# The last residual taken by tokens, keys' sums 30 steps later, whole tiles in the second feed-forward, and gathers that skip empty places

## The chip, the cores and the metric

One core of a Trainium2 chip runs the whole program in one launch. The time is that of the device, in microseconds (us), from start to end of the program. The kernel before takes 2077.78 us, the median of three runs (2077.6 to 2078.44). Engines: PE (TensorE, matrix products), DVE (VectorE), ACT (ScalarE), POOL (GpSimd), SP (SyncE, which issues nearly all loads).

## The reference

The input is 512 tokens of width 1024 in float32. The first block is attention over chunks, a short convolution, a mixture of 32 experts (two per token, 1024 choices in all) and a gated projection. The second block puts 16 meta tokens in front (528 tokens) and has two layers: a pooling mixer with a feed-forward, then grouped attention over a window with a feed-forward. After the first layer one normed input gives keys and values. What the change touches, cut to it:

```python
# experts: the rows of each expert, in blocks; places without a token have weight 0
xs = xn[row_tok].reshape(n_blk, BLK, d)
hdn = silu(xb @ w1[e]) * (xb @ w3[e]);  ys = hdn @ w2[e]
out = zeros((t, d)).at[row_tok].add(ys * row_w[:, None])

# each layer of the second block ends with
h  = rms_norm_2(hs, norm_ffn_pre[layer])
hs = hs + rms_norm_2(swiglu(h, w_gate_up[layer], w_down[layer]), norm_ffn_post[layer])
# rms_norm_2(y, g) = y / sqrt(mean(y*y) + 1e-6) * g, the mean over the 1024 channels of a token
if layer == 0:
    kv_in = rms_norm_2(hs, kv_norm); k = kv_in @ w_k + b_k; v = kv_in @ w_v + b_v
return hs[:, 16:]
```

Evaluated on its own inputs, the reference gives the 32 experts 50, 36, 28, 41, 36, 37, 32, 34, 20, 24, 25, 29, 27, 23, 26, 28, 44, 38, 29, 34, 37, 39, 31, 22, 35, 32, 28, 44, 28, 28, 26 and 33 of the 1024 choices.

## The kernel before, in words

**Layout.** Activations stand with channels on the 128 partitions and tokens along a row: hT is 8 blocks of 128 channels by 528 tokens. Products are made in three passes of fp32r (`nhi*whi`, `nlo*whi`, `nhi*wlo`), all at L426 in `tile`. One `tile` is one block of 128 output channels: for each of K blocks of inputs it loads a 128x128 weight and multiplies up to 512 tokens into one PSUM bank. In the second block the tokens are held as two halves; in layer 1 these are 256 and 256 tokens (RX), so a tile over both halves takes two banks and two products of 256 columns for each weight.

**Weights.** A unit is 128x1024 (eight 128x128 blocks). SP loads it into one of four raw buffers, ACT casts it to `whi` (L1962), DVE subtracts to get `wlo` (L1130). ACT and DVE do this in `feed`, inside their own copies of the loop over tiles: at block k of tile m, DVE feeds up to the unit in hand plus 2, ACT up to plus 3. A down product with 10 blocks per tile therefore asks for a new unit every 8 blocks.

**Side work.** Each engine has a list of generators (`Side`); `tile` calls `side.tick()` after every block of inputs but the last. So the norms between stages run step by step beside dense products, in an order that is fixed when the program is built: an engine that waits in a side step holds all that stands behind it, its next `feed` too.

**Norm after the downs.** The down products of the second half of the inputs (`fd1`) run for the first token half (r=0, 8 tiles of 10 blocks), then for the second (r=1). After r=0 `after(0)` puts a norm on the list of each engine. `pe_norm` waits a steps, takes the column sums of squares (`columns`, L835 and L836), waits b steps, and spreads the root over the partitions by products with a diagonal (`spread`, L857); (a, b) is LAG = (4, 6). Then 11 steps follow in which DVE scales y by gain and root (L1707), POOL (r=0, L2608) or DVE (r=1, L1712) adds it to hT and, in layer 0, ACT and DVE make `nhi` and `nlo` for the keys while ACT squares and POOL sums (L2547). In layer 0 the sums for the keys' root, `pe_norm("kv", 0, 4, 6)`, stand next on the list: their `columns` come at step 26 counted from the start of r=1.

**The end.** After layer 1, `pe_last` turns hT by 128x128 transposes (L1019) into token rows, ACT copies them out of PSUM (L2500) and SP stores them (L2801), eight stores of 256 KB in pieces of 1 KB. For r=0 this is beside the downs of r=1, for r=1 it is the tail.

**Experts.** Each expert has 64 places. For each pair of experts POOL gathers 128 token rows of 4 KB from HBM by the list `tix` (L2585); a place without a token holds 0, so token 0's row is fetched. SP streams the experts' weights, 96 loads of 2 MB, into nine slots; a slot is loaded again when its products are done. `tix` comes from one-hot products (L604) of `pat` (POOL) and `pb` (DVE), turned to int32 by DVE.

Of the kernel before, what the change touches and what calls it, by code (L numbers as in the profile page):

```python
# [9 lines left out]
ALU = mybir.AluOpType  # L10
# [3 lines left out]
D = 1024  # L14
S = 512
# [34 lines left out]
NRAW = NSP = 4  # L50

# [90 lines left out]
def _program(nc, ctx, T, out, marks):  # L142
# [123 lines left out]
    sl = [pl(f"sl{i}", [128, L]) for i in range(2)]  # L266
    assert pl.off <= nc.sbuf_usable_end
    XW = 4
# [130 lines left out]
    def tensor(e):  # L399
# [473 lines left out]
        def pe_ffn(l, rngs, off, nev, after):  # L873
# [135 lines left out]
        def pe_last(r):  # L1009
            yield from pe_post("fo1", r)  # L1010
            if r == 0:
                for _ in range(WAIT):
                    yield
            for hf in range(2):
                for i in (2 * r, 2 * r + 1):
                    b = take(("fin", i, hf), SIDE)
                    for k in range(4):
                        w.wait_ge(*at("h", "fo1", r, 4 * hf + k))
                        p = e.transpose(b[:, k * 128:(k + 1) * 128],  # L1019
                                        hT[:, 4 * hf + k, MT + i * 128:MT + (i + 1) * 128], ident)  # L1020
                    p.then_inc(*hit("pe_turn", ("turned out", i, hf)))
                    yield
# [33 lines left out]
    WAIT = 10  # L1056
# [12 lines left out]
    LAG = (4, 6)  # L1069
    JOIN = ("join_pe", "join_dve", "join_act", "join_pool", "join_sp")  # L1070
# [47 lines left out]
    def vector(e):  # L1118
# [168 lines left out]
        def dve_route():  # L1287
# [8 lines left out]
            e.tensor_scalar(c31, iota[:, 0:32], -1.0, 31.0, ALU.mult, ALU.add).then_inc(*hit("dve_route"))  # L1296
            w.wait_ge(*at("col", "n2", 0))
# [73 lines left out]
            dv(e.tensor_copy, tix[:], bk("by place", 0, n=NB // 2), ev=[("tix",)])  # L1371
# [10 lines left out]
            for n in range(2):  # L1382
                dv(e.tensor_copy, tcol[:, n, :], bk("by place", n, n=NB // 2), ev=[("free", "by place", n)])
# [295 lines left out]
        def columns(nm, r):  # L1679
# [5 lines left out]
            root(e, w, y, xm, u, "dve_root", nm, r)  # L1685
# [1229 lines left out]
```

## Time and profile before

| What | Value |
|---|---|
| Runs | 2077.6, 2077.78, 2078.44 us |
| The profiled execution's own time | 2076.99 us |
| Its span (first to last instruction) | 2075.2 us |
| Mean granted clock of TensorE | 0.963 |
| PE busy | 1914.2 us (92% of the span) |
| DVE, ACT, POOL busy | 961.8, 651.3, 194.5 us |
| HBM read, written | 349.38 MB, 4.19 MB |

A line of instructions gives a time, a duration, the engine, the line of the kernel, the operation, what it writes and reads with its shape, a count and, in brackets, how long the engine was idle before and what released it. "SPq" or "POOLq" is an engine's issuing queue. A view by stretches gives the busy time of each engine with its instructions, then the granted clock (1.00 is 2.4 GHz, 0.50 is 1.2 GHz), the DMA engines' share and GB/s. The matmuls are pipelined, so the time that one costs in a stream is the distance between two starts, not its duration.

### The profile page before, as it was taken

The page shows a single profiled execution, that of the slowest core. Times are in us where ns is not written, and L with a number is a line of the kernel's source. Part 1 is how long each engine was busy: PE and PEld are TensorE (multiplying, and loading weights), DVE is VectorE, ACT ScalarE, POOL GpSimd, SP SyncE. Part 2 cuts the span into 40 slices and gives each one's busy share as a digit, 9 for nine tenths or more (in the row PEclk, how much of TensorE's full clock was granted, in tenths as well). Part 3 has the DMA queues.
Part 4 walks back from the last instruction along what each step waited for, and adds up shares of the span by engine and source line. Part 5 has one row for each costly group of instructions (what it writes and reads, how often), then busy time and mean ns, then how long its engine had stood idle before and what let it go on. Part 6 is the DMA issues. An engine that isn't in the chain of part 4 may idle for free.

```text
span 2075.2 us, 33252 instructions
## 1 busy us (share of the span) xinstructions
PE 1914.2 (92%) x14370; PEld 1632.3 (79%) x14370; DVE 961.8 (46%) x1702; ACT 651.3 (31%) x1209; POOL 194.5 (9%) x178
## 2 busy tenths in 40 slices
PE   7999999989998898889699999997898789999997
PEld 5766788866665566569699999997766789999996
DVE  5655334223332232257963323357665674323355
ACT  6344323211010010055432222234555543222232
POOL 0011100100000000000300000014122410000012
PEclk9999999989999999999899999998999889999998
DMA  4221243589999999942112322243211333232242
GB/s 178 82 72 61 74 172 102 240 318 426 426 426 426 428 425 426 428 171 82 62 32 92 102 89 75 94 140 102 72 52 41 102 117 117 92 106 87 93 143 82
DMA packets 58087, 355.79 MB, mean 171 GB/s; under 512 B 6304, under 2 KB 8992, under 8 KB 45648
## 3 DMA queue, kind: packets, MB, share of 16 engines
q1 hardware_dynamic: 54112, 340.44, 42.7%
q0 software_dynamic: 3504, 12.73, 1.7%
q8 instruction: 116, 1.90, 0.4%
q10 hardware_dynamic: 320, 0.43, 0.1%
q14 instruction: 35, 0.29, 0.0%
HBM read 349.38 MB, written 4.19 MB: 170 GB/s over the span
## 4 chain that ended last, share of the span: by engine, by line
PE 72%; DVE 10%; DMA 10%; ACT 4%; issue 2%; POOL 2%; SPq 0%; DVEq 0%; ACTq 0%; POOLq 0%
PE bank L426 51%; DMA e<-in_we 9%; PE bank L631 7%; PE bank L653 4%; ACT SS L2442 1%; PE bank L474 1%; PE bank L664 1%; PE bank L780 1%; PE bank L665 1%; DVE wlo L1130 1%; DVE ztmp L1707 1%; POOL zacc L2547 1%; DVE SS L1847 1%; DVE sm L1854 1%; PE bank L618 1%
## 5 line engine op out<-in xcount | busy, mean ns | idle before, releaser
L426 PE MATMUL bank<-nhi,whi 128*128 128x256 f32 (+2 forms) x1472 | 424.9, 289 | 4.1 <-DVE nlo L1717 1.9
L426 PE MATMUL bank<-nhi,wlo 128*128 128x256 f32 (+2 forms) x1472 | 420.1, 285 | 0.0
L426 PE MATMUL bank<-nlo,whi 128*128 128x256 f32 (+2 forms) x1472 | 420.1, 285 | 0.0
L1130 DVE TENSOR_TENSOR wlo<-raw,whi 128x1024 fp32r<-128x1024 f32 x242 | 304.5, 1263 | 131.2 <-ACT whi L1962 127.4
L1962 ACT CAST whi<-raw 128x1024 fp32r<-128x1024 f32 x247 | 256.9, 1043 | 116.4 <-PE bank L426 93.1
L426 PEld LDWEIGHTS bank<-nhi,whi 128*128 128x128 f32 x1472 | 280.0, 190 | 9.1 <-DVE nlo L1717 2.5
L426 PEld LDWEIGHTS bank<-nlo,whi 128*128 128x128 f32 x1472 | 279.6, 190 | 0.9
L426 PEld LDWEIGHTS bank<-nhi,wlo 128*128 128x128 f32 x1472 | 279.1, 190 | 1.5
L631 PE MATMUL bank<-e,xT 128*64 128x256 f32 x2048 | 236.5, 384 | 0.8 <-DVE xT L1392 0.8
L631 PEld LDWEIGHTS bank<-e,xT 128*64 128x64 f32 x2048 | 142.9, 138 | 82.3 <-issue 15.1
L426 PE MATMUL bank<-ghi,whi 128*128 128x256 f32 (+1 forms) x704 | 201.1, 286 | 0.0
L426 PE MATMUL bank<-ghi,wlo 128*128 128x256 f32 (+1 forms) x704 | 199.8, 284 | 0.0
L426 PE MATMUL bank<-glo,whi 128*128 128x256 f32 (+1 forms) x704 | 199.7, 284 | 0.0
L653 PE MATMUL bank<-e,h 128*64 128x256 f32 x1024 | 117.2, 388 | 32.1 <-DMA e<-in_we 31.1
L653 PEld LDWEIGHTS bank<-e,h 128*64 128x64 f32 x1024 | 84.5, 140 | 63.7 <-issue 36.6
L426 PEld LDWEIGHTS bank<-ghi,whi 128*128 128x128 f32 x704 | 134.3, 191 | 0.0
L426 PEld LDWEIGHTS bank<-glo,whi 128*128 128x128 f32 x704 | 134.2, 191 | 0.0
L426 PEld LDWEIGHTS bank<-ghi,wlo 128*128 128x128 f32 x704 | 134.0, 190 | 0.0
L2547 POOL TENSOR_TENSOR zacc<-zacc,zq 128x256 f32<-128x256 f32 (+1 forms) x60 | 59.7, 996 | 775.2 <-ACT zq L2245 774.7
L1414 DVE SCALAR_TENSOR_TENSOR ylo<-bank,tcol,yhi 128x512 fp32r<-128x512 f32 x32 | 23.9, 750 | 233.0 <-ACT yhi L2137 233.0
L426 PE MATMUL bank<-xhi,whi 128*128 128x512 f32 x288 | 122.5, 425 | 0.8 <-DVE xlo L1152 0.8
L426 PE MATMUL bank<-xhi,wlo 128*128 128x512 f32 x288 | 113.7, 395 | 0.0
(343 smaller groups left out, 2969.1 us busy)
## 6 DMA issues: line engine op xcount, KB each, us to landing
e<-in_we SPq DMA_DIRECT2D x96, 2048.0 KB, 34.8
raw<-in_w_down SPq DMA_DIRECT2D x64, 512.0 KB, 3.3
raw<-in_w_gate SPq DMA_DIRECT2D x48, 512.0 KB, 3.3
raw<-in_w_up SPq DMA_DIRECT2D x48, 512.0 KB, 3.2
raw<-in_w_q SPq DMA_DIRECT2D x12, 512.0 KB, 4.4
B<-in_rel POOLq DMA_DIRECT2D x8, 512.0 KB, 4.2
raw<-in_w_gc SPq DMA_DIRECT2D x8, 512.0 KB, 3.3
raw<-in_w_ga SPq DMA_DIRECT2D x8, 512.0 KB, 4.1
```

The costliest lines, as they stand in the source:

```text
L426: i = e.matmul(o, a, x[:, k0 + k, c0:c1], start=(k == 0 and n == 0), stop=(k == j.K - 1 and n == 2))
L474: p = e.matmul(bs[i][:, 0:256], x[:, k, t], a, start=(k == 0 and n == 0), stop=(k == 7 and n == 2))
L618: i = e.transpose(b[:, k * 128:(k + 1) * 128], xg[0 if ov else p % 2][:, (4 * c + k) * 128:(4 * c + k + 1) * 128], ident)
L631: p = e.matmul(b[64 * hf:64 * hf + 64, 0:256], x[:, k, :], W[:, k, 256 * hf:256 * hf + 256], start=(k == 0), stop=(k == 7))
L653: i = e.matmul(b[64 * x:64 * x + 64, 256 * q:256 * q + 256], h2[x][:, 2 * (kc % 2) + kc // 2, :], W[x][:, kc, 512 * nh + 256 * q:512 * nh ...
L664: e.matmul(b[:], yhi[:, k * 128:(k + 1) * 128], pick[:], start=True, stop=False)
L665: e.matmul(b[:], ylo[:, k * 128:(k + 1) * 128], pick[:], start=False, stop=True).then_inc(*hit(f"pe_moe{ov}", ("spread y", p, k)))
L780: p = e.matmul(o, a, x[:, k, c0:c1], start=(k == 0 and n == 0), stop=(k == 7 and n == 2))
L1130: e.tensor_tensor(wlo[wslot(u)][:], raw[u % NRAW][:], whi[wslot(u)][:].bitcast(F32), ALU.subtract).then_inc(*hit("dve_low", ("lo", u)))
L1414: e.scalar_tensor_tensor(ylo[:, c], bk("y", p, nh), tcol[:, 1, p:p + 1], yhi[:, c].bitcast(F32), ALU.mult, ALU.subtract).then_inc(*hit(f"d ...
L1962: e.copy(whi[wslot(u)][:], raw[u % NRAW][:]).then_inc(*hit("act_high", ("hi", u)))
L2547: e.tensor_tensor(a, a, zq[marks.noted("sq", nm, r, k)][:, 0:c1 - c0], ALU.add).then_inc(*hit("pool_acc", ("acc", nm, r, k)))
```

## The change

Five parts.

1. **Empty places.** The list is built from token number minus 1024, and 1024 is added after the sum, so an empty place holds 1024. The gather has a bound of 511 and leaves rows beyond it out. POOL clears both gather buffers once, after `pb`, and the first gather waits for it.
2. **Keys' sums.** `pe_norm("kv", 0, 4, 6)` becomes `(34, 8)` on PE, DVE, ACT and POOL: `columns` at step 56 of the 72 of r=1, `spread` at step 64.
3. **Whole tiles.** In layer 1 the gate and up tiles from the fifth on, and the first downs (`fd0`), run over 512 tokens at once, into one bank. DVE's gate and up steps and ACT's copy of `fd0` are one of 512 instead of two of 256.
4. **h turned early.** During the downs of r=0 in layer 1, PE turns hT (8 groups of four transposes, one group each fifth step) and ACT copies them to `ho` (tokens on partitions).
5. **The sum turned apart.** POOL makes `gdiag`, eight 128x128 diagonals of the gain. PE multiplies y by them (float32), which turns and scales it at once; DVE takes the root as a column only (no diagonal, no spread, no copy of rb) and adds: `ho = turned * root + ho`, 128x512 each. SP stores from `ho` in pieces of 2 KB. DVE's eight scalings, the additions on POOL or DVE and ACT's copies at the end go.

```diff
-                    tile(J["fg", l, i], 0, ("fg", l, i), nhi, nlo, xrs, lambda k: [])
-                    tile(J["fu", l, i], 0, ("fu", l, i), nhi, nlo, xrs, lambda k: [])
+                    tile(J["fg", l, i], 0, ("fg", l, i), nhi, nlo, ALL if l else xrs, lambda k: [])
+                    tile(J["fu", l, i], 0, ("fu", l, i), nhi, nlo, ALL if l else xrs, lambda k: [])
...
-                        tile(J["fd", l, 0, 0], m, ("fd0", l, m), ghi, glo, rr,
+                        tile(J["fd", l, 0, 0], m, ("fd0", l, m), ghi, glo, [(0, (MT, L))] if l else rr,
...
+            if l:
+                side.add(pe_turn_h())
...
-                side.add(pe_norm("kv", 0, 4, 6))
+                side.add(pe_norm("kv", 0, *KV_LAG))
...
-        def pe_last(r):
-            yield from pe_post("fo1", r)
-            if r == 0:
-                for _ in range(WAIT):
-                    yield
-            for hf in range(2):
-                for i in (2 * r, 2 * r + 1):
-                    b = take(("fin", i, hf), SIDE)
+        def pe_turn_h():
+
+            w.wait_ge(*at("out", "fu", 1, 21))
+            for i in range(4):
+                for hf in range(2):
+                    b = take(("h out", i, hf), SIDE)
                     for k in range(4):
-                        w.wait_ge(*at("h", "fo1", r, 4 * hf + k))
+                        w.wait_ge(*at("h", "mp1", i // 2, 4 * hf + k))
                         p = e.transpose(b[:, k * 128:(k + 1) * 128],
                                         hT[:, 4 * hf + k, MT + i * 128:MT + (i + 1) * 128], ident)
+                    p.then_inc(*hit("pe_turn", ("turned h", i, hf)))
+                    yield from nothing(5)
+
+        def pe_last(r):
+
+            def turn(hf):
+                for i in (2 * r, 2 * r + 1):
+                    b = take(("fin", i, hf), DENSE if r and hf else SIDE)
+                    for k in range(4 * hf, 4 * hf + 4):
+                        w.wait_ge(*at("y", "fo1", r, k))
+                        p = e.matmul(b[:, (k % 4) * 128:(k % 4 + 1) * 128], yT[:, k, MT + i * 128:MT + (i + 1) * 128],
+                                     gdiag[:, k, :], start=True, stop=True)
                     p.then_inc(*hit("pe_turn", ("turned out", i, hf)))
-                    yield
+
+            w.wait_ge(*at("gdiag"))
+            if r == 0:
+                yield from nothing(LAG[0])
+            turn(0)
+            yield
+            columns("fo1", r)
+            yield
+            if r == 0:
+                yield from nothing(9)
+            turn(1)
+            yield
...
+    KV_LAG = (34, 8)
...
         def dve_last(r):
-            yield from dve_post("fo1", r, "ffn_post", 1, None, None, 0)
-            for _ in range((WAIT if r == 0 else 0) + 4):
-                yield
+            if r == 0:
+                yield from nothing(LAG[0])
+            yield
+            column_root("fo1", r)
+            yield
+            for hf in range(2):
+                if r == 0 and hf:
+                    yield from nothing(9)
+                for i in (2 * r, 2 * r + 1):
+                    o = ho[:, i, 512 * hf:512 * hf + 512]
+                    w.wait_ge(*at("turned out", i, hf))
+                    w.wait_ge(*at("free", "h out", i, hf))
+                    e.scalar_tensor_tensor(o, bk("fin", i, hf), rcol[:, 0, i + 1:i + 2], o, ALU.mult, ALU.add).then_inc(
+                        *hit("dve_post", ("free", "fin", i, hf)))
+            yield
...
+            w.wait_ge(*at("xg clear"))
...
             e.indirect_dma_start(out=xg[q][:], out_offset=None, in_=n2d,
-                                 in_offset=bass.IndirectOffsetOnAxis(ap=tix[:, p:p + 1], axis=0)).then_inc(
+                                 in_offset=bass.IndirectOffsetOnAxis(ap=tix[:, p:p + 1], axis=0), bounds_check=S - 1,
+                                 oob_is_err=False).then_inc(
                                      *dma(f"d_xg{q}{ov}", ("xg", p)))
...
+        w.wait_ge(*at("pb"))
+        for n in range(2):
+            e.memset(xg[n][:], 0.0).then_inc(*hit("pool_route", *([("xg clear",)] if n else [])))
...
+            if l:
+                g = VEC["ffn_post"] + 8
+                e.tensor_tensor(gdiag[:], ident.unsqueeze(1).to_broadcast([128, 8, 128]),
+                                vec[:, g:g + 8].unsqueeze(2).to_broadcast([128, 8, 128]), ALU.mult).then_inc(
+                                    *hit("pool_post", ("gdiag",)))
...
-                    e.dma_start(out[i * 128:(i + 1) * 128, 512 * hf:512 * hf + 512].rearrange("p (a c) -> p a c", a=2),
-                                out_tile(i, hf)).then_inc(*dma(f"d_out{i}{hf}", ("stored", i, hf)))
+                    e.dma_start(out[i * 128:(i + 1) * 128, 512 * hf:512 * hf + 512],
+                                ho[:, i, 512 * hf:512 * hf + 512]).then_inc(*dma(f"d_out{i}{hf}", ("stored", i, hf)))
```

## Rows read from the trace of the kernel before

**Rows 1.** The page's chain that ended last, by line, shares of the span.
```profile
PE bank L426 51%; DMA e<-in_we 9%; PE bank L631 7%; PE bank L653 4%; ACT SS L2442 1%; PE bank L474 1%; PE bank L664 1%; PE bank L780 1%; PE bank L665 1%; DVE wlo L1130 1%; DVE ztmp L1707 1%; POOL zacc L2547 1%; DVE SS L1847 1%; DVE sm L1854 1%; PE bank L618 1%
```

**Rows 2.** Busy time by stretches of the experts: us, engines, clock, DMA share, GB/s.
```profile
467.00:500.00 33.00, 33.00 (x272) 21.48 (x269) 11.09 (x19) 4.11 (x9) 1.88 (x2) 1.00 1.00 426
...
592.00:860.00 268.00, 240.41 (x1925) 162.20 (x1926) 75.97 (x129) 25.31 (x54) 6.57 (x7) 0.99 1.01 426
```

**Rows 3.** DMA issues: the gathers, their count and median us to landing.
```profile
xg<-n_scratch,tix POOLq DMA_INDIRECT x16, 11.4
```

**Rows 4.** Timeline of the routing's end and a later gather: start us, us, engine, line, what.
```profile
421.37 1.04 POOL L2678 TENSOR_TENSOR scr<-scr,cst 128x512 f32<-128x512 f32 x1 [19.87 <-DVE scr L1291]
...
422.91 0.56 DVE L1291 TENSOR_TENSOR scr<-scr,rows 128x384 f32<-128x384 f32 x1
...
427.30 1.24 POOL L2585 DMA_INDIRECT xg<-n_scratch,tix  x1 [4.89 <-DVE tix L1291]
...
433.13 1.97 PE L618 MATMUL bank<-cst,xg 128*128 128x128 f32 x8 [2.25 <-DMA xg<-n_scratch,tix]
...
496.04 0.94 POOL L2585 DMA_INDIRECT xg<-n_scratch,tix  x1 [26.03 <-PE bank L618]
```

**Rows 5.** Timeline of PE in layer 0's downs, second token half.
```profile
1405.67 0.28 PE L426 MATMUL bank<-ghi,wlo 128*128 128x256 f32 x1
1418.29 0.56 PE L835 MATMUL bank<-cst,zacc 128*128 128x1 f32 x2 [12.34 <-ACT zq L2245]
...
1444.11 0.28 PE L835 MATMUL bank<-cst,zacc 128*128 128x1 f32 x2
```

**Rows 6.** The same stretch on DVE: the next weight unit.
```profile
1418.28 1.22 DVE L1130 TENSOR_TENSOR wlo<-raw,whi 128x1024 fp32r<-128x1024 f32 x1
```

**Rows 7.** Stretches after that stall.
```profile
1418.20:1424.40 6.20, 6.11 (x28) 6.14 (x29) 4.27 (x17) 0.88 (x1) 0.00 (x0) 0.50 0.26 85
```

**Rows 8.** Layer 1's tiles of two halves, a stretch of them.
```profile
1696.00:1840.00 144.00, 144.00 (x1231) 144.00 (x1230) 60.22 (x87) 44.90 (x63) 0.00 (x0) 1.00 0.35 118
```

**Rows 9.** Timeline of PE in products of 512 columns: block 1, then block 2.
```profile
249.66 0.39 PE L426 MATMUL bank<-xhi,whi 128*128 128x512 f32 x1
...
261.90 0.39 PE L426 MATMUL bank<-xhi,whi 128*128 128x512 f32 x1
...
1608.59 0.40 PE L426 MATMUL bank<-nlo,whi 128*128 128x512 f32 x1
...
1619.98 0.39 PE L426 MATMUL bank<-nhi,wlo 128*128 128x512 f32 x1
```

**Rows 10.** Timeline of PE in layer 1's downs, second token half.
```profile
2021.87 0.28 PE L835 MATMUL bank<-cst,zacc 128*128 128x1 f32 x2
...
2025.51 0.71 PE L857 MATMUL bank<-dg,cst 128*128 128x128 f32 x4
2025.97 0.37 PE L426 MATMUL bank<-ghi,whi 128*128 128x256 f32 x1
...
2034.54 0.60 PE L1019 MATMUL bank<-cst,hT 128*128 128x128 f32 x4
2034.89 0.36 PE L426 MATMUL bank<-ghi,whi 128*128 128x256 f32 x1
...
2038.50 0.33 PE L1019 MATMUL bank<-cst,hT 128*128 128x128 f32 x1 [2.00 <-POOL hT L2608]
```

**Rows 11.** Timeline of PE's last dense product and its column sums.
```profile
2057.05 0.28 PE L426 MATMUL bank<-ghi,wlo 128*128 128x256 f32 x1
2058.84 0.35 PE L835 MATMUL bank<-cst,zacc 128*128 128x1 f32 x2 [1.51 <-ACT zq L2245]
```

**Rows 12.** Timeline of DVE and ACT in the tail.
```profile
2062.06 0.43 DVE L1690 TENSOR_TENSOR dg<-cst,rcol 128x256 f32<-128x256 f32 x1
...
2071.63 0.59 ACT L2500 COPY yT<-bank 128x512 f32<-128x512 f32 x1 [0.27 <-PE bank L1019]
```

**Rows 13.** The page's group of DVE's step of 512 columns out of PSUM.
```profile
L1414 DVE SCALAR_TENSOR_TENSOR ylo<-bank,tcol,yhi 128x512 fp32r<-128x512 f32 x32 | 23.9, 750 | 233.0 <-ACT yhi L2137 233.0
```

More of the change, by code:

```diff
@@ L50 @@
 NRAW = NSP = 4
+NOROW = 1024
 class Marks:
@@ L266, in _program @@
     sl = [pl(f"sl{i}", [128, L]) for i in range(2)]
+    gdiag = pl("gdiag", [128, 8, 128])
     assert pl.off <= nc.sbuf_usable_end
+    ho = Place(EA)("ho", [128, 4, D])
     XW = 4
@@ L1370, in dve_route @@
             w.wait_ge(*at("by place", 0))
-            dv(e.tensor_copy, tix[:], bk("by place", 0, n=NB // 2), ev=[("tix",)])
+            dv(e.tensor_scalar, tix[:], bk("by place", 0, n=NB // 2), float(NOROW), None, ALU.add, ev=[("tix",)])
             dv(e.tensor_tensor, R["pw"], pb, wgt[:].rearrange("p a b -> p (a b)").unsqueeze(2).to_broadcast([128, 8, 48]),
@@ L1381, in dve_route @@
             w.wait_ge(*at("by place", 1))
-            for n in range(2):
-                dv(e.tensor_copy, tcol[:, n, :], bk("by place", n, n=NB // 2), ev=[("free", "by place", n)])
+            dv(e.tensor_scalar, tcol[:, 0, :], bk("by place", 0, n=NB // 2), float(NOROW), None, ALU.add,
+               ev=[("free", "by place", 0)])
+            dv(e.tensor_copy, tcol[:, 1, :], bk("by place", 1, n=NB // 2), ev=[("free", "by place", 1)])
         def dve_tokens(p, w, ov=""):
@@ L1677, in mixed_post, with column_root @@
                                                *hit("dve_norm", ("n", "fp0", r, k)))
-        def columns(nm, r):
+        def column_root(nm, r):
             n0, n1 = cols(nm, r)
@@ L1685, in columns @@
             root(e, w, y, xm, u, "dve_root", nm, r)
+            w.wait_ge(*at("root", nm, r))
+        def columns(nm, r):
+            column_root(nm, r)
+            n0, n1 = cols(nm, r)
             m0 = max(n0, 1)
-            w.wait_ge(*at("root", nm, r))
             if n0 == 0:
@@ L1746, in up, with gate_all, up_all @@
                     *hit("dve_out", ("free", *key, r), ("act", l, i, r)))
+            def gate_all(i, key):
+                for r in range(2):
+                    w.wait_ge(*at("free", "rb", nev, r))
+                    if i - 2 < FIRST:
+                        w.wait_ge(*at("g", l, i - 2, r))
+                w.wait_ge(*at("out", *key))
+                if i - 2 >= FIRST:
+                    w.wait_ge(*at("g", l, i - 2))
+                e.tensor_tensor(sl[i % 2][:, t0:t1], bk(*key, 0), rb[:, t0:t1], ALU.mult).then_inc(
+                    *hit("dve_out", ("free", *key, 0), ("gated", l, i, 0), ("gated", l, i, 1)))
+            def up_all(i, key):
+                w.wait_ge(*at("silu", l, i, 0))
+                w.wait_ge(*at("out", *key))
+                e.tensor_tensor(sl[i % 2][:, t0:t1], sl[i % 2][:, t0:t1], bk(*key, 0), ALU.mult).then_inc(
+                    *hit("dve_out", ("free", *key, 0), ("act", l, i, 0), ("act", l, i, 1)))
             def split(i, x0, x1, *r):
@@ L1767, in dve_ffn @@
                     tile(J["fg", l, i], 0)
-                    for r in range(2):
+                    if l:
+                        gate_all(i, ("fg", l, i))
+                    for r in range(0 if l else 2):
                         gate(i, r, ("fg", l, i))
                     tile(J["fu", l, i], 0)
-                    for r in range(2):
+                    if l:
+                        up_all(i, ("fu", l, i))
+                    for r in range(0 if l else 2):
                         up(i, r, ("fu", l, i))
@@ L2366, in act_ffn @@
                         w.wait_ge(*at("out", "fd0", l, m))
-                        for r, (x0, x1) in enumerate(rngs):
+                        for r, (x0, x1) in enumerate([(t0, t1)] if l else rngs):
                             e.copy(yT[:, m, x0:x1], bk("fd0", l, m, r, n=x1 - x0)).then_inc(
@@ L2371, in act_ffn @@
             nm = f"fo{l}"
+            if l:
+                side.add(act_turn_h())
             for r in range(2):
@@ L2488, in act_after1, with act_turn_h @@
         def act_after1(r):
-            side.add(act_last(r))
-        def act_last(r):
-            yield from act_post("fo1", r, None, None, 0)
-            if r == 0:
-                for _ in range(WAIT):
-                    yield
-            for hf in range(2):
-                for i in (2 * r, 2 * r + 1):
-                    w.wait_ge(*at("turned out", i, hf))
-                    w.wait_ge(*at("post x", "fo1", r, 7))
-                    e.copy(out_tile(i, hf), bk("fin", i, hf).rearrange("p (a c) -> p a c", a=2)).then_inc(
-                        *hit("act_out", ("free", "fin", i, hf)))
-                    yield
+            pass
+        def act_turn_h():
+            for i in range(4):
+                for hf in range(2):
+                    w.wait_ge(*at("turned h", i, hf))
+                    e.copy(ho[:, i, 512 * hf:512 * hf + 512], bk("h out", i, hf)).then_inc(
+                        *hit("act_out", ("free", "h out", i, hf)))
+                    yield from nothing(5)
         act_load()
@@ L2631, in pool_after0 @@
             if r == 0:
-                side.add(nothing(11))
+                side.add(nothing(sum(KV_LAG) + 1))
         def pool_kv():
```

18 lines of the change are left out of this document (9 added, 9 removed).

## The prediction

> **What bounds the kernel now.** I read the page's chain first: dense products of PE at L426 hold half of it, the wait for experts' weights 9%, and no group of the other engines over 1% [rows 1]. So a microsecond counts only where it is PE's, the weight stream's, or in the tail. The stretches of the experts show which of the two holds there: the DMA engines are full (share 1.00 and 1.01, 426 GB/s) from 467 us on, while from 592 us PE is idle for 28 of 268 us [rows 2]. In the timeline of PE I then looked for holes: one of 12.34 us before the keys' sums in layer 0 [rows 5], holes before the transposes in layer 1's downs [rows 10], and the tail behind the last dense product [rows 11, 12]. The profiled execution took 2076.99 us, 0.79 less than the median of the runs; the sum is made against it and 0.8 is added at the end.
>
> **1. Empty places.** 16 gathers of 128 rows of 4096 B are 8.39 MB, of which 1024 rows are empty (2048 places, 1024 choices, no expert over its 64). The first three are issued before the stream is full, so 13 count: 13 x 64 rows x 4096 B = 3.41 MB, at 426 GB/s 8.0 us [rows 2, 3]. That is one end, with the missing rows spread evenly over the 16 DMA engines. The other end is 0: if one engine carried only low places, which every expert fills (20 to 50 of 64), it would have as much to do as before, and a load is whole only when its slowest engine is done. I take 6.0 us, nearer to the even case, since on average half of each expert's places fall away but not evenly. PE does not take the bound over: it has 10% of slack there [rows 2], and this takes 2%.
> The Trainium skill (DMA: Bandwidth & Descriptors, The descriptor swizzle) gives the mapping: partitions 4e to 4e+3 and 32 above them go to one engine, the upper 64 partitions to the other eight engines. With the reference's counts the fullest engine would then carry 69 of its 104 rows in those 13 gathers and save 35 x 4096 B at 26.6 GB/s, 5.4 us; no row of this trace tells the engines apart.
>
> The two clears: `pb` is there at 423.5 us (422.91 + 0.56), the first gather is issued at 427.3, so POOL has 3.8 us [rows 4]. Its nearest operation is 1.04 us for 512 elements; twice 1024 would be 4.2 us at that rate and 0.4 late, and a write without reads should be less: 0, bound 0.4. A gather with a bound may cost POOL more or, with half the rows, land sooner than 5.8 us (427.30 to 433.13): 0, bounds -1 to +1; the later ones are issued a pair ahead, some 27 us (0.94 us and 26.03 us of waiting for PE) [rows 4], and hide it. The small edits on DVE stand in its waits: 0.
>
> **2. Keys' sums.** PE stops at 1405.79 (1405.67 and one product of 0.117; step 26, block 29 of 80 of r=1) and goes on at 1418.29 [rows 5]. What it waits for ends late because the 11 steps of scaling, adding, splitting and summing run on DVE, POOL and ACT until 1418.3 whether PE waits or not: the releaser is ACT's square [rows 5]. With `columns` at step 56 PE runs on, but the next thing late is the weight. DVE's `feed` asks for unit 5 of these downs at its own block 24, which stands behind step 21, the last keys' step: it starts at 1418.28, without idle time before it, and takes 1.22 us, ready at 1419.50 [rows 6]. PE needs unit 5 at block 40: 33 more products of 0.117 us [rows 8] bring it there at 1409.65. So the hole shrinks from 12.34 to 9.85 us and moves; it does not go.
> Then, as before, the granted clock is 0.50 for at least 6.2 us after the stall [rows 7]: 30 of the 120 products left cost 0.213 (256 columns at 1.2 GHz), 6.4 us; 90 cost 10.5; the column sums (12 instructions) and the spread 2.1 at full clock. End of r=1: 1419.50 + 19.0 = 1438.5. Before, it ended near 1442.2 (1444.11 less 15 products of 272 columns, 1.9) [rows 5]. Gain 3.7 us; 2.8 if half clock lasts 8 us, 5.2 if 3.5, about half of what is seen. The spread comes 9 blocks, 3.2 us, after sums of 1.3, so 4.5 us from their start; in the tail the diagonal was there 3.7 us from it (2058.84 to 2062.49) [rows 11, 12]: no new wait.
>
> **3. Whole tiles.** 18 gate and 18 up tiles of 8 blocks and 8 downs of 12 blocks, three passes: 864 + 288 = 1152 pairs of 256 columns become products of 512. A pair costs 2 x 0.1170 = 0.2340 us (144 us, 1231 products) [rows 8]. A product of 512 columns cost 0.2267 in block 1 (54 in 12.24 us), but 0.232 over the very operand `nhi` in block 2 (49 in 11.39 us) [rows 9]. I take the latter, as the operand and its spacing stay: 1152 x 0.002 = 2.3 us; ends 1.0 and 8.4. DVE and ACT lose work here, hidden under a PE without holes: 0.
>
> **4. h turned early.** A group of four transposes pushed the next product from 0.117 to 0.35 us behind its start, and that product lasted 0.36 in place of 0.28: 0.43 us [rows 10]. Eight groups beside r=0: +3.4 us on PE. ACT's eight copies (0.59 each [rows 12]) are hidden by PE's 28 us of r=0.
>
> **5. The sum turned apart.** r=1 of layer 1 began at 2020.1 (2021.87 less 15 products) and ended at 2057.17: 37.05 us for 240 products that need 28.1 [rows 10, 11]. In it are the column sums, the spread, four groups of transposes, the waits for POOL's additions and the half clock behind them. After: 28.1, column sums 0.9, and four groups of four float32 products. Such a product is two instructions of 0.115 (2025.51 to 2025.97 for four) [rows 10], so 0.92 + 0.08 a group, 4.0 in all: 33.0, a gain of 4.0. DVE's new steps (root at step 5, additions at 6 and 15) stand before its unit 4 and wait for PE's own steps of the same number, so no weight is late. `gdiag` (128x1024 on POOL) lies in POOL's idle time.
> Tail: before, 15.05 us from 2057.17 to the end of the last copy (2072.22) and 2.98 to the end of the span [rows 12]. After: two turned groups, 16 x 0.115 = 1.84, before the column sums, which so begin 0.3 late (they began at 2058.84); root ready at 2062.35; four additions of 128x512 out of PSUM at 0.75 [rows 13], ended at 2065.35. The other two groups are turned under the root, even at half clock (3.4 us from 2060.0). Then the same 2.98. Gain 6.9; 5.0 if PE is cold and late for the last pair.
>
> **Sum.** -6.0 - 3.7 - 2.3 + 3.4 - 4.0 - 6.9 = -19.5: 2057.5 in the profile's time, 2058.3 us in that of the runs. The terms' own ends: gathers 0 to 8, keys 2.8 to 5.2, whole tiles 1 to 8.4, h 3 to 4, r=1 and tail 8.5 to 11.5.
>
> **Rivals.**
> *The keys' hole goes entirely.* For it: the program puts the sums behind the end of the steps. Against: DVE's order of feeds, worked out above. It would give the hole and its half clock back, some 12 us more: 2046. Chance 0.10.
> *The gathers save nothing.* For it: a row left out may still cost its engine a descriptor, or one engine keeps all its rows. Against: counts around half. 2058.3 + 6 = 2064.3. Chance 0.17.
> *Slower: the bound makes the gather dear.* If POOL's gather with a bound checks row by row, its landing could grow from 5.8 to over 26 us. The first would hold up PE and the weights' slots for the excess in full; later ones hide up to 15 us (27 less 11.4) [rows 3, 4]. From 20 us of excess on, the change is not faster: 2079. For it: POOL builds the list in software and the trace has no gather of this form; against: a whole gather now keeps POOL 0.94 to 1.24 us [rows 4]. Chance 0.04.
> *Whole tiles at block 1's pace* (0.2267): 6 us more, 2052. Chance 0.12. The forecast itself has 0.57.
>
> **Numbers.** 2058.3; range 2049 to 2067, which leaves out most of the first rival and of the slow one, and holds both disputed sizes. No difference means within 0.2%, 4 us. Faster 0.94, same 0.02, slower 0.04.
>
> **What would show it.** A hole of about 10 us at block 40 of layer 0's r=1 whose releaser is DVE's L1130 in place of 12.3 before L835; 0.232 us a product in layer 1; half the gathered rows and a stream that ends some 6 us sooner after its start; no wait for POOL in layer 1's downs; 11 us from the last dense product to the end in place of 18. Wrong would be: another releaser or no hole at all in layer 0, PE waiting for `xg` beyond the first, or a wait for `gdiag` or `turned out` in front of a weight feed.

## Result and the profile after

The kernel after takes 2051.35 us (median of 4 runs, 2050.37 to 2057.19), the kernel before 2078.11 beside it (4 runs); ratio 0.9877, 95% interval 0.986 to 0.9894. The forecast was 2058.3 (2049 to 2067). The profiled execution took 2052.12 us with a span of 2050.3, 24.9 less than before's.

The page's chain that ended last, by line (L429, L634 and L656 are before's L426, L631 and L653), and its line on the queue of the gathers (packets, MB, share of 16 engines):

```profile
PE 75%; DVE 10%; DMA 8%; ACT 4%; issue 2%; POOL 1%; DVEq 0%; SPq 0%; ACTq 0%; POOLq 0%
PE bank L429 52%; PE bank L634 8%; DMA e<-in_we 7%; PE bank L656 4%; ACT SS L2512 1%; PE bank L667 1%; PE bank L477 1%; PE bank L668 1%; PE bank L783 1%; DVE wlo L1157 1%; DVE SS L1903 1%; DVE sm L1910 1%; PE bank L621 1%; POOL zacc L2608 1%; PE bank L494 1%
...
q0 software_dynamic: 3504, 8.54, 1.2%
```

The weights' share of the chain fell from 9 to 7% [rows 1]. The queue moves 4.19 MB less than the 12.73 of before, in the same 3504 packets: a row left out is still a small packet.

**Experts.** The stretch that answers to [rows 2] (us, engines, clock, DMA share, GB/s), the routing's end in the timeline [rows 4], and what PE waited for from 440 to 910 us, first in the kernel after, then before (us in total, times, longest):

```profile
592.00:860.00 268.00, 248.81 (x1970) 165.17 (x1968) 77.75 (x133) 25.54 (x54) 6.93 (x7) 0.97 1.01 426
```
```profile
422.93 1.04 POOL L2746 TENSOR_TENSOR scr<-scr 128x512 f32<-128x512 f32 x1 [19.85 <-DVE scr L1318]
425.09 1.85 POOL L2751 MEMSET xg<- 128x1024 f32 x2 [1.11 <-DVE scr L1318]
429.44 1.10 POOL L2647 DMA_INDIRECT xg<-n_scratch,tix  x1 [2.50 <-DVE scr L1318]
...
434.87 1.54 PE L621 MATMUL bank<-cst,xg 128*128 128x128 f32 x6 [2.43 <-DMA xg<-n_scratch,tix]
```
```profile
PE bank L656 <- DMA e<-in_we: 21.3, 8, 4.4
```
```profile
PE bank L653 <- DMA e<-in_we: 31.1, 10, 4.9
```

The DMA engines stay full at 426 GB/s, so the stream still sets the time, but it has less to carry: PE waits 9.8 us less. The clears end at 426.94, 2.5 us before the gather: they cost nothing. The gather's issue is 2.14 us later than before's, of which 1.56 were there at `pat` already. The other 0.58 stand on POOL between `tix` and the issue: `tix` was ready at 428.57 (427.02 before), 0.87 us ahead of the gather in place of 0.28. From issue to PE it takes 5.4 us (5.8 before), from `tix` to PE 6.3 (6.1), so the bound is not dear.

**Keys' sums.** PE and DVE around the stall [rows 5, 6], and the stretch behind it [rows 7]:

```profile
1405.58 0.28 PE L429 MATMUL bank<-ghi,wlo 128*128 128x256 f32 x1
...
1415.42 0.55 PE L429 MATMUL bank<-ghi,whi 128*128 128x256 f32 x1 [9.56 <-DVE wlo L1157]
```
```profile
1413.63 0.50 DVE L1751 SCALAR_TENSOR_TENSOR nlo<-hT,vec,nhi 128x272 fp32r<-128x272 f32 x1 [1.20 <-ACT nhi L2382]
1414.05 1.22 DVE L1157 TENSOR_TENSOR wlo<-raw,whi 128x1024 fp32r<-128x1024 f32 x1
```
```profile
1415.40:1418.90 3.50, 3.48 (x17) 3.50 (x18) 3.43 (x6) 2.15 (x4) 1.50 (x2) 0.53 0.66 173
```

The hole is where the forecast put it, behind DVE's low part of unit 5, which stands behind the last step for the keys. The half clock behind it lasted 3.5 us here, 6.2 or more before.

**Layer 1.** The whole tiles, then the second downs' two halves, before and after [rows 8, 10], and a group of h's transposes:

```profile
1722.39:1991.88 269.49, 269.49 (x2307) 269.49 (x2306) 94.44 (x137) 73.77 (x100) 0.00 (x0) 1.00 0.29 97
1991.88:2020.12 28.24, 28.24 (x242) 28.24 (x241) 18.82 (x27) 13.59 (x18) 7.24 (x6) 1.00 0.52 171
2020.12:2057.17 37.05, 33.61 (x270) 32.93 (x268) 24.47 (x44) 12.60 (x20) 14.82 (x14) 0.95 0.29 98
```
```profile
1708.62:1975.55 266.93, 266.93 (x1155) 216.37 (x1153) 92.17 (x102) 73.31 (x92) 0.00 (x0) 1.00 0.32 97
1975.55:2007.35 31.80, 31.80 (x274) 31.80 (x273) 18.83 (x26) 17.80 (x26) 7.25 (x6) 1.00 0.51 151
2007.35:2040.05 32.70, 32.70 (x283) 32.70 (x282) 20.34 (x39) 10.15 (x15) 6.29 (x6) 1.00 0.34 112
```
```profile
1975.91 0.60 PE L1022 MATMUL bank<-cst,hT 128*128 128x128 f32 x4
1976.26 0.36 PE L429 MATMUL bank<-ghi,whi 128*128 128x256 f32 x1
1976.46 0.28 PE L429 MATMUL bank<-glo,whi 128*128 128x256 f32 x1
```

1152 products in 266.93 us are 0.2317 each. A group takes 0.55 us in place of one product's 0.12 (1975.91 to 1976.46): 0.43, eight times. In the last stretch PE is busy throughout, at full clock, where before it idled 3.4 us.

**Tail.** PE, DVE and the stores [rows 11, 12]:

```profile
2040.05 1.95 PE L1034 MATMUL bank<-gdiag,yT 128*128 128x128 f32 x16
2041.83 0.28 PE L838 MATMUL bank<-cst,zacc 128*128 128x1 f32 x2
...
2042.64 2.03 PE L1034 MATMUL bank<-gdiag,yT 128*128 128x128 f32 x16
```
```profile
2044.98 2.73 DVE L1980 SCALAR_TENSOR_TENSOR ho<-bank,rcol,ho 128x512 f32<-128x512 f32 x4
```
```profile
out<-ho SPq DMA_DIRECT2D x4, 256.0 KB, 2.1
```

10.26 us from the last dense product's end at 2040.05 to the span's end, in place of 18.02.

**The ledger.** Dense products are counted in PE's order, so both programs can be cut at the same ones. Lengths in us, each from the starts of two products in the profile (the last from the last product's end to the span's end):

| stretch | before | after | difference | forecast |
|---|---|---|---|---|
| to product 504 (block 1) | 227.45 | 229.03 | +1.58 | 0 |
| routing and experts, to 1248 | 679.31 | 672.50 | -6.81 | -6.0 |
| to 1776 (layer 0's gates) | 130.88 | 131.86 | +0.98 | 0 |
| to 4548 | 362.05 | 362.03 | -0.02 | 0 |
| layer 0's downs, second half, to 4752 | 42.52 | 37.98 | -4.54 | -3.7 |
| keys and attention of layer 1, to 5100 | 169.66 | 165.36 | -4.30 | 0 |
| to the first whole tile | 110.52 | 109.86 | -0.66 | 0 |
| whole tiles | 269.49 | 266.93 | -2.56 | -2.3 |
| second downs, first half | 28.24 | 31.80 | +3.55 | +3.4 |
| second downs, second half | 37.05 | 32.70 | -4.35 | -4.0 |
| behind the last dense product | 18.02 | 10.26 | -7.76 | -6.9 |

The changed stretches sum to -22.5, those that nothing changed in to -2.4. Of the latter, attention is the large one. There the clock tells. The whole stretch of the keys and attention, before and after:

```profile
1442.21:1611.87 169.66, 151.47 (x1006) 116.74 (x1005) 105.33 (x234) 90.64 (x258) 35.30 (x26) 0.94 0.16 57
```
```profile
1433.40:1598.76 165.36, 145.86 (x1006) 112.39 (x1005) 105.15 (x234) 90.45 (x258) 35.30 (x26) 0.98 0.19 58
```

By these clocks PE was at half clock for some 20 us of it before and for 7 after. Two stretches of before at part clock, and the one after that answers to the second:

```profile
1486.00:1506.00 20.00, 17.11 (x82) 10.82 (x82) 11.67 (x30) 11.96 (x38) 4.24 (x3) 0.74 0.08 27
1600.00:1607.00 7.00, 6.06 (x30) 5.04 (x30) 1.08 (x4) 3.41 (x8) 1.90 (x1) 0.51 0.01 2
```
```profile
1586.00:1596.00 10.00, 7.15 (x60) 5.51 (x59) 2.89 (x9) 5.79 (x17) 1.89 (x1) 1.00 0.13 49
```

The same stall stands in both just ahead of the second, before and after:

```profile
1600.94 1.98 PE L976 MATMUL bank<-PT,V 128*64 128x128 f32 x16 [2.86 <-ACT PT L2431]
```
```profile
1590.67 1.09 PE L981 MATMUL bank<-PT,V 128*64 128x128 f32 x16 [2.85 <-ACT PT L2501]
```

Before, half clock follows it and costs 2.8 us, after it does not. Why is open.

### The profile page after: what moved, and what is told of

Read it like the earlier page. It is cut to its first block, busy times and chain, and to the rows that moved or that the text cites. A ratio compares the mean times of both kernels' runs of the same rounds, so it can differ in the third digit from the quotient of the medians.

```text
span 2050.3 us, 30975 instructions
## 1 busy us (share of the span) xinstructions
PE 1909.2 (93%) x13274; PEld 1576.3 (77%) x13274; DVE 952.0 (46%) x1649; ACT 649.9 (32%) x1199; POOL 190.0 (9%) x173
## 3 DMA queue, kind: packets, MB, share of 16 engines
q0 software_dynamic: 3504, 8.54, 1.2%
HBM read 349.38 MB, written 4.19 MB: 172 GB/s over the span
## 4 chain that ended last, share of the span: by engine, by line
PE 75%; DVE 10%; DMA 8%; ACT 4%; issue 2%; POOL 1%; DVEq 0%; SPq 0%; ACTq 0%; POOLq 0%
PE bank L429 52%; PE bank L634 8%; DMA e<-in_we 7%; PE bank L656 4%; ACT SS L2512 1%; PE bank L667 1%; PE bank L477 1%; PE bank L668 1%; PE bank L783 1%; DVE wlo L1157 1%; DVE SS L1903 1%; DVE sm L1910 1%; PE bank L621 1%; POOL zacc L2608 1%; PE bank L494 1%
## 5 line engine op out<-in xcount | busy, mean ns | idle before, releaser
L429 PE MATMUL bank<-nhi,whi 128*128 128x256 f32 (+2 forms) x1184 | 375.8, 317 | 3.7 <-DVE yT L1955 1.6
L429 PE MATMUL bank<-nlo,whi 128*128 128x256 f32 (+2 forms) x1184 | 372.9, 315 | 0.0
L429 PE MATMUL bank<-nhi,wlo 128*128 128x256 f32 (+2 forms) x1184 | 372.8, 315 | 0.0
L429 PEld LDWEIGHTS bank<-nhi,whi 128*128 128x128 f32 x1184 | 225.4, 190 | 21.6 <-DVE nlo L1751 2.2
L634 PE MATMUL bank<-e,xT 128*64 128x256 f32 x2048 | 237.0, 385 | 0.8 <-DVE xT L1422 0.8
L429 PEld LDWEIGHTS bank<-nlo,whi 128*128 128x128 f32 x1184 | 225.0, 190 | 13.6
L429 PEld LDWEIGHTS bank<-nhi,wlo 128*128 128x128 f32 x1184 | 224.8, 190 | 13.6
L634 PEld LDWEIGHTS bank<-e,xT 128*64 128x64 f32 x2048 | 143.2, 138 | 82.5 <-issue 14.9
L429 PE MATMUL bank<-ghi,whi 128*128 128x272 f32 (+2 forms) x608 | 184.7, 304 | 9.6 <-DVE wlo L1157 9.6
L429 PE MATMUL bank<-ghi,wlo 128*128 128x272 f32 (+2 forms) x608 | 183.4, 302 | 0.0
L429 PE MATMUL bank<-glo,whi 128*128 128x272 f32 (+2 forms) x608 | 183.4, 302 | 0.0
L656 PE MATMUL bank<-e,h 128*64 128x256 f32 x1024 | 119.5, 393 | 22.5 <-DMA e<-in_we 21.3
L1444 DVE SCALAR_TENSOR_TENSOR ylo<-bank,tcol,yhi 128x512 fp32r<-128x512 f32 x32 | 23.9, 750 | 225.6 <-ACT yhi L2205 225.6
L656 PEld LDWEIGHTS bank<-e,h 128*64 128x64 f32 x1024 | 83.7, 142 | 57.0 <-issue 29.6
L429 PEld LDWEIGHTS bank<-ghi,whi 128*128 128x128 f32 x608 | 115.4, 190 | 14.3 <-issue 9.7
L429 PE MATMUL bank<-xhi,whi 128*128 128x512 f32 x288 | 123.1, 427 | 0.9 <-DVE xlo L1179 0.9
L429 PEld LDWEIGHTS bank<-glo,whi 128*128 128x128 f32 x608 | 115.3, 190 | 4.3
L429 PEld LDWEIGHTS bank<-ghi,wlo 128*128 128x128 f32 x608 | 115.1, 189 | 4.1
L429 PE MATMUL bank<-xhi,wlo 128*128 128x512 f32 x288 | 114.4, 397 | 0.0
```

Of the source, the lines that this page charges most:

```text
L429: i = e.matmul(o, a, x[:, k0 + k, c0:c1], start=(k == 0 and n == 0), stop=(k == j.K - 1 and n == 2))
L634: p = e.matmul(b[64 * hf:64 * hf + 64, 0:256], x[:, k, :], W[:, k, 256 * hf:256 * hf + 256], start=(k == 0), stop=(k == 7))
L656: i = e.matmul(b[64 * x:64 * x + 64, 256 * q:256 * q + 256], h2[x][:, 2 * (kc % 2) + kc // 2, :], W[x][:, kc, 512 * nh + 256 * q:512 * nh ...
L1444: e.scalar_tensor_tensor(ylo[:, c], bk("y", p, nh), tcol[:, 1, p:p + 1], yhi[:, c].bitcast(F32), ALU.mult, ALU.subtract).then_inc(*hit(f"d ...
```

## Experiments

Each run's time is the median, beside before's on the same chip. The ratio and its interval are estimated from all executions and can lie 0.2% off the quotient of the two medians. Since the executions of one kernel differ by up to 10.7 us, the stretches of the profiles carry the verdicts; each of these is one execution.

**Each part alone, on the kernel before.** The edits are the diff's own hunks, one part in each kernel.

> The kernel before with part 1 alone (rows for empty places left out, the bound, the clears). Theory (the weight stream sets the time of the experts, and rows not moved shorten it): last expert product 6 to 7 us sooner, less 0.2 to 2 us of a later first gather; 2071.5 against 2078.1. Rival (the gain of the profile after in the experts, 6.8 us from its start, comes from somewhere else, or a row left out still costs its engine): under 2 us, 2076 to 2078. In both the rest of the program keeps its distances, except for half-clock phases of TensorE, which may fall elsewhere.

> The kernel before with part 2 alone (column sums for the keys at step 56 and spread at 64). Theory: the hole of 12.3 us in layer 0's second half of downs becomes one of 9.7 at block 40, released by DVE's low part of unit 5; 4.5 us less at its end, 2073.6. Rival (the gain measured there was due to what part 1 changed before): under 2 us. If the 4.3 us that layer 1's attention lost in the profile after, by half clock that did not come, hang on the time at which this stage ends, they appear here too: 2069.

> The kernel before with part 3 alone (gate, up and first downs of layer 1 in products of 512 columns). Theory: 1152 products at 0.2317 us in place of 2304 at 0.1170: 2.6 us, 2075.5. Rival (the gain is more, since DVE and ACT have a third fewer instructions there and hold nothing up later): 4 us or more, 2074.

> The kernel before with parts 4 and 5 alone (h turned early, the sum of the downs turned apart, the root as a column). Theory: +3.55 in the first half of the downs, -4.35 in the second, -7.8 behind the last dense product: 2069.5. Rival (the half-clock phase of the tail comes and goes, and the tail's gain of 7.8 in place of the forecast 6.9 is chance): 2070.5 to 2072.

| kernel | us | before | ratio, interval | its stretches against before's |
|---|---|---|---|---|
| gathers_alone | 2071.09 | 2078.48 | 0.9964, 0.9952 to 0.9977 | experts -7.9 |
| keys_alone | 2071.65 | 2078.48 | 0.9970, 0.9958 to 0.9981 | downs of layer 0 -4.6 |
| whole_tiles_alone | 2072.21 | 2078.48 | 0.9971, 0.9960 to 0.9983 | whole tiles -2.56 |
| last_sum_alone | 2070.57 | 2078.48 | 0.9955, 0.9943 to 0.9968 | +3.57, -4.35, -7.75 |

The four gains sum to 28.4 us, where all together brought 26.8. Every stretch gives its term back to 0.1 us, the experts to 1.1. The experts' stretch took 671.4 to 672.5 us in the eight profiles with the bound and the usual order of places, and 679.3 to 681.1 in the four without it. In keys_alone PE waits for the weight as in the kernel after:

```profile
PE bank L426 <- DVE wlo L1131: 9.6, 1, 9.6
```

Whole_tiles_alone gained 6.3 and not 2.6; in its profile the excess stands outside its code: block 1 was 1.85 shorter and attention 2.7, against +1.2 in the last half of the downs. The rival that DVE and ACT hold less up has no stretch to show. Yet the interval of its six executions, 3.5 to 8.3 us, leaves out 2.6, so by the total this rival is not refuted, and why all six are so quick is open. The total of last_sum_alone also fell among its rival's 2070.5 to 2072; there the tail's gain, the same in every profile that has the part (10.3 us left), refutes it.

Attention of layer 1 lasted 165.4 to 169.8 us in the ten profiles of kernels that leave its code and rows as they are; the 165.4 is the kernel after's, so part of the 24.9 between the two profiles is luck. Keys_alone ended the stage ahead 4.4 us sooner than before and has 168.1, not 165.4: the end of the stage ahead alone does not bring the 4.3.

**Which engine carries which place.** One more row of numbers takes the counter's place in `pa`: the column's place number, dealt in another order. The line is put in once for each kernel, with one of the two endings.

```
+            e.tensor_copy(R["perm"].rearrange("p (a b d) -> p a b d", a=2, b=8),
+                          iota[:, 0:64].rearrange("p (a d b) -> p a b d", a=2, d=4))   # spread
+                          iota[:, 0:64].rearrange("p (b a d) -> p a b d", b=8, a=2)    # packed
```

> The kernel after, with the places of an expert dealt to the partitions in another order: filled ones go to partitions 0, 4, 8, ... first, so that each group of 32 partitions gives every fourth partition its turn. Same rows and bytes in all. Theory A (a DMA engine serves groups of four neighbouring partitions, 32 apart, and a load is whole when its fullest engine is done): by the counts the fullest engine carries 56 rows in place of 69 of 104 in the last 13 gathers, 2.0 us less in the experts; 2049.4 against 2051.4 of the kernel after. Theory B (only the sum of the bytes counts): no change, 2051.4.

> The kernel after, with the places dealt so that the filled ones fill partitions 0 to 3 and 32 to 35, then 4 to 7 and 36 to 39, and so on. Same rows and bytes in all. Theory A (engines go by groups of four partitions, 32 apart): the engine of the first groups carries all its 104 rows in the last 13 gathers, so nothing is saved against the kernel before and the experts take 5.4 us more than after (up to 8 if the gain of 6.8 measured there goes entirely); 2056.8 to 2059. Theory B (only the sum of the bytes counts): no change, 2051.4.

Packed: 2060.44 against 2076.90 (0.9907, 0.9886 to 0.9927), 1.4 above theory A's range; experts 678.97 us, 6.5 more than after, inside it, and 0.3 less than before. Spread: 2054.90 (0.9872, 0.9851 to 0.9894); experts 672.99, 0.5 more than after. Median landing of the experts' weights between 424 and 900 us, in the order before, after, packed, spread:

```profile
e<-in_we SPq DMA_DIRECT2D x87, 2048.0 KB, 36.1
```
```profile
e<-in_we SPq DMA_DIRECT2D x88, 2048.0 KB, 34.0
```
```profile
e<-in_we SPq DMA_DIRECT2D x88, 2048.0 KB, 35.6
```
```profile
e<-in_we SPq DMA_DIRECT2D x88, 2048.0 KB, 34.1
```

PE waited 29.1 us for them in packed and 18.7 in spread:

```profile
PE bank L656 <- DMA e<-in_we: 29.1, 10, 5.0
```
```profile
PE bank L656 <- DMA e<-in_we: 18.7, 9, 3.2
```

Same rows and bytes, and the gain is gone: theory B falls. Which partitions are filled decides. The Trainium skill (DMA: Bandwidth & Descriptors, The descriptor swizzle) states that in a transfer to 128 partitions one engine serves four neighbouring partitions and the four 32 above them. Packed agrees; places_spread does not bear out that the fullest engine alone sets the time. By that rule the estimates of the gain are 0 us for packed, 5.4 after and 7.4 for spread (104, 69 and 56 of 104 rows on the fullest engine, at 426/16 GB/s); measured against before were 0.3, 6.8 (7.9 with the part alone) and 6.3. A's 2.0 did not come, and why is open.

The 2.6 us of waits that PE had less in spread are no sign of a quicker stream: gathers_alone, in the usual order, has 19.0. From the experts' first product to their last, PE was granted half clock for about 26 us in spread and 24 in gathers_alone, 18 after; beside a full stream a slower PE would wait less, which is argued and not tested.

**The hole before the keys.** Paced gives each step three blocks; the other moves POOL's additions to DVE. The edits, shortened:

```
-    KV_LAG = (34, 8)
+    KV_LAG = (12, 8)
...
+                if (nm, r) == ("fo0", 0):        # behind each step, on PE, DVE, ACT, POOL
+                    yield from nothing(2)
```
```
-            yield from post_steps(nm, r, lambda s: v1(name, 8 * l + s), nev, g, off, r)
+            yield from post_steps(nm, r, lambda s: v1(name, 8 * l + s), nev, g, off, r or nm == "fo0")
...
-                if r == 0 and 1 <= s < 9:                  # POOL
+                if r == 0 and nm != "fo0" and 1 <= s < 9:
```

> The kernel after, with each of the 11 steps that prepare the keys (scale, add, split, square) given three blocks of the downs in place of one, on all engines; the sums stay at step 57 and the spread 8 later. Theory A (the hole of 9.7 us at block 40 is the order on DVE: unit 5's low part behind all steps): no hole at block 40, what is left is what DVE has too much in the 28 us, at most 5 us in smaller holes later, and less half clock behind them; this stage 5 to 9 us shorter, about 2044. Theory B (the steps' chain over POOL and DVE is too long wherever it stands): the hole moves to the sums, and its length stays within 2 us of 9.7; 2050 to 2052.

> The kernel after, with the 8 additions of the residual for r=0 of layer 0 done by DVE (as for r=1) in place of POOL. Theory C (POOL at work slows DVE: L1741 and L1751 took 0.5 us when POOL idled and 1.0 when it worked, so the steps last 16 us by contention): DVE's steps are 16 of 0.5 and 8 additions of 0.5, with a unit's low part and a pair of downs' additions 14 us in place of 16.8 to unit 5's low part: hole 7 us in place of 9.7, about 2048.7. Theory D (POOL's chain has nothing to do with it, DVE only gets 8 more instructions): hole 2 to 4 us longer, 2053.4 to 2055.4.

Paced: 2050.07 against 2076.90 (0.9871, 0.9851 to 0.9891); this stretch 34.86 us against after's 37.98. Additions on DVE: 2053.91 (0.9881, 0.9862 to 0.9899), stretch 36.86. What PE waited for in it, paced first:

```profile
PE bank L429 <- DVE wlo L1158: 4.7, 2, 2.6
```
```profile
PE bank L429 <- DVE wlo L1157: 8.1, 1, 8.1
```

Theory A holds for the cause: with the weights' low parts between the steps the hole falls from 9.6 to 4.7 us, in two places, both still behind a low part and none at the sums, though the steps are the same. Its size it missed: the stage is 3.1 us shorter and not 5 to 9, and the total is 2050 and not 2044. C holds in sign, at half its size (8.1, not 7), and its total gained nothing over the kernel after (2053.91, forecast 2048.7). A DVE step with POOL's additions and the POOL instruction beside it, then DVE without them:

```profile
1403.55 1.01 DVE L1751 SCALAR_TENSOR_TENSOR nlo<-hT,vec,nhi 128x272 fp32r<-128x272 f32 x1
1404.47 1.01 DVE L1741 SCALAR_TENSOR_TENSOR ztmp<-yT,vec,rb 128x272 f32<-128x272 f32 x1
...
1404.21 0.96 POOL L2671 TENSOR_TENSOR hT<-hT,ztmp 128x272 f32<-128x272 f32 x1
```
```profile
1394.63 0.50 DVE L1741 SCALAR_TENSOR_TENSOR ztmp<-yT,vec,rb 128x272 f32<-128x272 f32 x1
1395.05 0.43 DVE L1746 TENSOR_TENSOR hT<-hT,ztmp 128x272 f32<-128x272 f32 x1
```

One step is 0.50 us alone and 1.0 beside POOL. The Trainium skill (SBUF — State Buffer, SBUF: two separate sides) states that a DVE operation with two SBUF inputs and a GpSimd one that reads SBUF take one pair of ports in turn, each for its whole instruction. The rows agree with it, but do not tell a lock from a shared rate.

**The pace of a product.** Rows of g laid 2336 B apart; then all of layer 1's operands laid alike; then these rows with the paced steps and DVE's additions together; then n's rows alone, with the paced steps. The edits, shortened:

```
-    ghi = pl("ghi", [128, 12, L], F32R)
+    ghi = pl("ghi", [128, 12, 584], F32R)      # stepped; aligned: 576, placed 128 B on
...
+    nhi1 = Place(EA)("nhi1", [128, 8, S], F32R)  # aligned: n of layer 1, rows 2048 B apart
```

> The kernel after, with the rows of ghi and glo 2336 B apart in place of 2112 (nothing else changed), so that in the first downs of layer 1 the 12 blocks of a tile read 512 columns from starts that are 224, 0, 32, 64, 96, 128, 160, 192, 224, 0, 32 and 64 above a multiple of 256 B. Theory F (a product's pace hangs on where its moving operand starts: in the profile after, the blocks of the gates that start 96 above a multiple of 256 are quicker, the others stand at 232 to 233 ns, and block 1's operands all start at 96): only the fifth block is near 227 to 230 ns, the other eleven 233; mean 232.7. Rival G (the pace is that of the row distance or of the operand's length, and block 1 is quicker for another reason): no block stands out, and the mean stays at 231.7 or moves for all alike.

> The kernel after, with the operands of layer 1 (attention's output product, gates, ups, downs) laid so that every block starts 96 B above a multiple of 256 B: rows 2048 B apart for n, 2304 B for g. Theory F: 0.2267 us a product of 512 columns in place of 0.2317 and 0.1134 in place of 0.1172 for 256: 1248 x 0.005 + 1056 x 0.0038 = 10.3 us in layer 1, and 1.2 in layer 0's downs, whose second half then starts at 96 too (the first at 32); 2051.4 - 11.5 = 2039.9. Rival G: within 1 us of the kernel after, 2050.4 to 2052.4.

> The kernel after with the operands of layer 1 laid as in the run before this one, the keys' steps given three blocks each, and r=0's additions of layer 0 done by DVE. Theory: the terms add: 11.5 us for the rows, 3.1 for the pacing and 1 to 2 for the additions (less contention with POOL, so less of the 4.7 us of holes that the pacing left); 2035 to 2036. Rival: DVE, with 8 additions more among the paced steps, holds PE up longer than in the paced kernel (holes over 4.7 us); 2038 to 2040.

> The kernel after with two things: the keys' steps at three blocks each (additions of r=0 left to POOL, as the paced kernel had them), and rows of n 2048 B apart in layer 1 alone (g keeps 2112 B). Theory: the paced steps keep their 3.1 us in layer 0's downs, where DVE's additions cost all_together 2.1 of them; 864 products of 512 columns in gates and ups go from 0.2317 to 0.2267 (-4.3), 384 products of 256 columns ahead of them get slower by 0.4 in all, and the downs keep the times that they had in the kernel after (no +0.45 and +0.56); 2051.4 - 3.1 - 3.9 = 2044.4. Rival (the pace hangs on all of layer 1's operands, g included, or the paced kernel's gain was chance): 2047 or more.

Stepped (2054.17, one run) had no single quick block: its first downs stayed at 0.2318 a product, and the block at 96 took 228, 232 and 228 ns (the middle one reads glo, which lies 128 B off), its neighbour at 128 took 231, 228 and 228. So the start alone isn't the rule, and on this run rival G was right. Aligned: 2053.29 against 2077.22 (0.9880, 0.9865 to 0.9895), but the whole tiles:

```profile
1715.92:1977.07 261.15, 261.15 (x1155) 216.23 (x1153) 92.21 (x102) 73.33 (x92) 0.00 (x0) 1.00 0.32 99
1977.07:2009.32 32.25, 32.25 (x273) 32.25 (x272) 18.82 (x26) 17.78 (x26) 7.23 (x6) 1.00 0.46 150
2009.32:2042.60 33.28, 33.28 (x283) 33.28 (x282) 20.36 (x39) 10.15 (x15) 6.30 (x6) 1.00 0.37 110
```

261.15 over 1152 is 0.2267, block 1's pace, 5.8 us less. Products of 256 columns went the other way, to a flat 0.120: the downs lost 0.45 and 0.56 us, and the 333 of the gates and ups ahead of the whole tiles that follow one another without a gap went from 0.1182 to 0.1199 each, 0.6 us. F forecast them quicker, and is wrong there. The total of 2053.29 is far from F's 2039.9 and doesn't show the 5.8; in that profile attention took 4.2 us more than after's and the stretch of the keys 1.5. Whether that holds for the other executions no profile shows.

All_together: 2046.43 against 2077.22 (0.9853, 0.9839 to 0.9866), above both forecasts (2035 to 2036, rival 2038 to 2040), which built on F's 11.5. Its rival was right on the keys: two holes, the longer 3.6, and 36.92 us for a stretch that took 34.86 when paced alone.

```profile
PE bank L437 <- DVE wlo L1166: 5.0, 2, 3.6
```

Paced_and_rows: 2046.30 against 2076.92 (0.9855, 0.9841 to 0.9868), span 2044.4. Its stretch of the keys took 34.90 us, its whole tiles:

```profile
1706.95:1969.61 262.66, 262.66 (x1155) 216.26 (x1154) 92.21 (x102) 73.37 (x92) 0.00 (x0) 1.00 0.33 98
```

That is 4.3 less than after's 266.93, and 3.1 less for the keys: both terms came. The total is 1.9 above the forecast of 2044.4 and 0.7 below the rival's 2047. The ratio's interval overlaps that of the kernel after, so what it gains beyond that kernel rests on the stretches.

## Why the prediction was right

**Empty places.** Forecast -6.0, measured -6.8 in the pair and -7.9 alone. That the bytes left out of a full stream are the gain, and that it hangs on the partitions, is shown by packed, which takes it away. The mapping's 5.4, by the fullest engine, was too little, and the even case's 8.0 nearer than thought. The clears and the first gather's latency were free, as said.

**Keys' sums.** Forecast a hole of 9.85 at block 40 behind DVE's low part, measured 9.56 there. -4.54 and not -3.7, because half clock lasted 3.5 us, the short end of the bounds; in places_spread and rows_aligned, with the same order of work here and the same hole (9.57), it lasted 5.6 and 6.1 behind it, and the stretch was 1.2 and 1.5 longer. So the 0.8 beyond the forecast hangs on the execution: six profiles with this order of work have 37.9 to 39.5 us. By the forecast's own sum 3.5 us of half clock would have given 5.2; the other 0.7 is not traced. The rival that the hole goes entirely fell for the reason given, DVE's order; pacing the steps took 4.9 of its 9.6.

**Whole tiles.** 0.232 a product forecast, 0.2317 measured, -2.56 for -2.3. The rival at 0.2267 failed on how the operand lies, which the change kept (rows 2112 B apart); laid 2048 and 2304 B apart at one alignment, the same 1152 products took 0.2267.

**h early.** +3.4 forecast, +3.55 measured, both by 0.43 a group; the last 0.1 is an estimate's rest.

**The sum turned apart.** r=1 -4.35 for -4.0, with no wait for POOL or the root. Tail 10.26 for 11.1: the term was mis-sized by three small amounts. The root was ready 4.93 us behind the last dense product (5.18 taken), the four additions took 2.73 (3.0), the stores and the end 2.60 (2.98). Whether the last comes from pieces of 2 KB no run tests.

**The rest.** The terms' errors make 3.0 of the 5.4 us by which the profile beat the sum. The other 2.4 fell where nothing was changed (+1.6, +1.0, -4.3 and -0.7) and are luck: over the profiles these stretches move by such amounts with no change of their code, block 1 from 225.6 to 229.2 us. In the medians the gain is 26.8 and not 24.9: the profiled execution before lay 1.1 below its median, the one after 0.8 above. Gathers that save nothing, a dear bound and a slower kernel had no sign in the trace.

## What to carry to other kernels

Read where the waiting engine's next need stands in its feeder's own order: a stall that is "removed" moves to the next item behind the same steps, and interleaving the feeds with them shortened it most (9.6 to 4.7 us). Bytes saved in a saturated stream may save nothing (packed), so look which partitions become empty. Cut both traces at the same instruction counts before believing a total: a gain of 5.8 us in one stretch did not show in a median here, and the stretch showed it to 0.1. And cut several profiles, since stretches that nothing changed moved by up to 4.4.

## What was not expected of the hardware

- The pace of float32r products of 512 columns hangs on how their operand's rows lie: 0.2267 us with rows a multiple of 256 B apart in rows_aligned, 0.2317 with 2112 B. It is neither the row distance alone (layer 1's queries, rows 2048 B apart, stood at 0.233: 34 steps from start to start in 7.93 us) nor the start alone (stepped). With 256 columns the aligned rows were slower, 0.120 against 0.1172. The rule behind it stays open.
- The same code at the same place ran with or without half clock behind the same stall (2.86 and 2.85 us), and one stretch that nothing changed took 165.4 to 169.8 us over ten profiles.
- A gathered row that is out of bounds still shows as a packet of 4 B: 1280 such between 420 and 900 us, 256 before. In the trace's packet records one takes 9 ns, a whole row 168.
